# Input projection of a hybrid pooling and DeltaNet block: seven half-size products per 256 weight columns in place of eight

## The chip, the core and the metric

The kernel runs on one core of a Trainium2 chip. The metric is the device time of one execution in microseconds (us). Each engine of the core works through its own instruction stream in order: TensorE (PE; its weight loads are listed as PEld), VectorE (DVE), ScalarE (ACT), GpSimd (POOL) and SyncE (SP), which here only issues DMAs. They meet at semaphores.

## What is computed

The reference runs one layer over 528 positions (16 learned meta tokens ahead of 512 tokens) of width 2048, all in float32. Cut to what matters:

```
xn = rmsnorm(h, norm_w)
proj = xn @ w_in                      # 528 x 2048 times 2048 x 14368
u_pool, z_pool, q, k, v, z_dn, b, a, gate_pool, gate_dn = split(proj)
y_pool = causal_multiscale_pool(u_pool, pool_mix, pool_scale) * silu(z_pool)
qkv    = causal_depthwise_conv_silu(concat(q, k, v), conv_w)    # 4 taps
y_dn   = chunk_gated_delta_rule(l2norm(q), l2norm(k), v, beta, g), then gated rmsnorm with silu(z_dn)
merged = sigmoid(gate_pool) * (y_pool @ w_pool_out) + sigmoid(gate_dn) * (y_dn @ w_dn_out)
out    = rmsnorm((h + merged @ w_o)[16:], final_norm_w)
```

The column groups of the projection are u and z of the pooling branch (1024 each), q, k, v and z of the delta branch (2048 each, 16 heads of 128), and two gates (2048 each).

## The kernel before

**Precision.** Every large product is made of three passes in a rounded float32 form: each operand is a high part plus a low part, and TensorE adds high times high, low times high and high times low. xh and xl hold the high and low parts of the normalised x, [128, 16, 528] each, transposed. Of the weights wh and wl hold the two parts. ACT makes a high part (a copy, `split_hi`, L868) and DVE the low one (raw minus high, `split_lo`, L1208).

**Input projection.** It goes in 56 blocks of 256 weight columns: for each of four pooling groups a u and a z block (8), for each of eight pairs of heads a k, q, v and z block (32), and 16 gate blocks. One block loads 2048 x 256 weights in two DMAs of 1 MB, and `window` (L530 does each matmul) runs four windows: two halves of 128 output channels by two halves of 1024 rows, each of eight row tiles. A tile is three passes. The z and gate blocks want only 512 positions and take one matmul of 512 columns for each pass; u, k and v take 256 and 272 (or 256 and 260 for q) columns, since 528 don't fit one bank. That is 96 or 192 matmuls in a block. Weights are split in pieces of two row tiles, two windows (48 or 24 matmuls) ahead of their use.

**Between the matmuls** lie hooks, one after every two row tiles. Through them all engines carry the delta rule of pair d (`delta(d, m)`, m from 0 to 52) while the projection of pair d+1 runs; that of the last pair runs under the first four gate blocks. Its steps come in this order: decay factors, the Gram matrices of k (m = 3, 4), 16x16 block inverses on DVE alone (m = 14 to 18, lines L1427 to L1443, called W here), the assembly of the inverse of each chunk (m = 29 to 34), the recurrence over four chunks (m = 35 to 46), output norms (m = 48 to 52). The convolution is four DVE operations of 528 columns for each head of k, q and v (`convolve`, L1373 and L1376), and silu follows on ACT. POOL fetches the row sums of the gates for pair d (L1720, L1722), subtracts (L1731), later stores the result zst of the pair (L1735), and at once goes on to the rows of the next pair.

**After the projection** come two stages that the change leaves as they are but for addresses and the first loads: B, eight steps of 144 matmuls of 512 columns with the branch outputs, and C, 768 matmuls with w_o, then residual and norm.

## Time and profile before

| | us |
|---|---|
| runs (median of 3; lowest, highest) | 1962.79 (1962.67, 1963.48) |
| profiled execution: span from first to last instruction | 1960.8 |
| PE busy in the span | 1931.4 (99%) |
| DVE busy | 921.4 (47%) |
| ACT busy | 726.0 (37%) |
| granted TensorE clock, mean | 0.997 |

The profiled execution is known by its span; the time of a run also holds what lies around the span, and the median is 2.0 us above it. Matmuls overlap in the listing: one of 512 columns is listed with some 390 ns, but the next starts sooner. So the spacing of starts gives the price, not the mean duration. The page of the profile has busy times, the chain that ended last and the costliest groups; the views of the trace give rows for a stretch of time.

### The profile page before, as it was taken

Reading aid. Unit: us, or ns where it says so; the run is one execution under the profiler, and the core shown is the slowest. Engines: PE = TensorE matmul, PEld = TensorE weight load, DVE = VectorE, ACT = ScalarE, POOL = GpSimd, SP = SyncE. Lnnn points to the kernel's source line nnn. Section 1 sums busy time; section 2 is a strip of 40 time slices with the busy share of each in tenths; the row PEclk is TensorE's granted clock in tenths of the full one; section 3 lists DMA queues with packets and bytes.
Section 4 is the critical chain, followed back from the end, with each engine's and each line's share of the span. In section 5 each row is a group of like instructions: output and inputs, shape, how many; then the busy total and the mean of one; then the engine's idle time right before and its main releaser. Section 6 shows DMA issues by size and latency. Waiting matters only on the chain.

```text
span 1960.8 us, 35753 instructions
## 1 busy us (share of the span) xinstructions
PE 1931.4 (99%) x13729; PEld 1724.3 (88%) x13729; DVE 921.4 (47%) x2315; ACT 726.0 (37%) x2136; POOL 78.3 (4%) x105
## 2 busy tenths in 40 slices
PE   5999999999999999999999999999999999999998
PEld 5888899999999999999999988888888888888886
DVE  6333343656556466555646654322224444335332
ACT  5422223435353443535345353323234322224232
POOL 4000000000000000000000000000000000000000
PEclk8999999999999999999999999999999999999999
DMA  6133342433333242333334144333443534347302
GB/s 222 59 103 102 102 134 88 119 95 86 95 120 90 87 124 69 96 111 100 91 107 123 44 131 127 119 107 128 134 162 134 186 118 139 118 139 279 108 22 86
DMA packets 221302, 225.73 MB, mean 115 GB/s; under 512 B 33665, under 2 KB 197978, under 8 KB 220522
## 3 DMA queue, kind: packets, MB, share of 16 engines
q1 hardware_dynamic: 158898, 180.17, 28.1%
q10 hardware_dynamic: 55944, 22.63, 4.6%
q0 software_dynamic: 6336, 21.08, 3.4%
q8 instruction: 102, 1.67, 0.4%
q14 instruction: 22, 0.18, 0.0%
HBM read 199.65 MB, written 25.30 MB: 115 GB/s over the span
## 4 chain that ended last, share of the span: by engine, by line
PE 97%; ACT 1%; DVE 1%; issue 0%; POOL 0%; DMA 0%; ACTq 0%; SPq 0%; DVEq 0%
PE pj L530 82%; PE pg L530 10%; PE pt L530 3%; PE pt L679 1%; PE pg L781 0%; POOL xl L1696 0%; DVE fst L1233 0%; ACT xsquare L908 0%; DMA xt<-in_meta_tokens 0%; PE pj L574 0%; DVE xl L1239 0%; ACT wh L868 0%; DVE xt L1246 0%; ACT L1041 0%; ACT L1070 0%
## 5 line engine op out<-in xcount | busy, mean ns | idle before, releaser
L530 PE MATMUL pj<-xh,wh 128*128 128x512 f32 (+3 forms) x2688 | 735.1, 328 | 3.2 <-DVE wl L1208 3.1
L530 PE MATMUL pj<-xh,wl 128*128 128x512 f32 (+3 forms) x2688 | 712.4, 319 | 0.0
L530 PE MATMUL pj<-xl,wh 128*128 128x512 f32 (+3 forms) x2688 | 712.3, 319 | 0.0
L1208 DVE TENSOR_TENSOR wl<-raw,wh 128x256 fp32r<-128x256 f32 x896 | 344.2, 421 | 603.0 <-ACT wh L868 601.5
L530 PEld LDWEIGHTS pj<-xh,wh 128*128 128x128 f32 x2688 | 446.9, 189 | 43.2 <-DVE wl L1208 3.4
L530 PEld LDWEIGHTS pj<-xh,wl 128*128 128x128 f32 x2688 | 448.4, 188 | 35.9
L530 PEld LDWEIGHTS pj<-xl,wh 128*128 128x128 f32 x2688 | 448.8, 189 | 33.9 <-issue 1.0
L868 ACT ACTIVATE wh<-raw 128x256 fp32r<-128x256 f32 x896 | 307.0, 410 | 64.7 <-issue 45.0
L868 ACT ACTIVATE wh<-rawb 128x256 fp32r<-128x256 f32 (+1 forms) x224 | 85.0, 437 | 217.0 <-PE pj L530 189.8
L530 PE MATMUL pj<-yl,wh 128*128 128x512 f32 x384 | 149.5, 389 | 0.0
L530 PE MATMUL pj<-yh,wl 128*128 128x512 f32 x384 | 149.5, 389 | 0.0
L530 PE MATMUL pj<-yh,wh 128*128 128x512 f32 x384 | 149.4, 389 | 0.0
L1559 DVE TENSOR_TENSOR wl<-rawb,wh 128x256 fp32r<-128x256 f32 x192 | 69.5, 419 | 94.6 <-ACT wh L868 94.6
L1376 DVE SCALAR_TENSOR_TENSOR stg<-xin,convcur,stg 128x528 f32<-128x528 f32 x144 | 109.4, 760 | 0.2
L868 ACT ACTIVATE xin<-pj 128x512 f32<-128x512 f32 (+2 forms) x128 | 34.1, 336 | 154.3 <-PE pj L530 131.5
L1070 ACT ACTIVATE stg<-pj 128x512 f32<-128x512 f32 x32 | 19.1, 598 | 184.9 <-PE pj L530 184.9
L530 PEld LDWEIGHTS pj<-yl,wh 128*128 128x128 f32 x384 | 72.1, 188 | 15.1
L530 PEld LDWEIGHTS pj<-yh,wl 128*128 128x128 f32 x384 | 72.1, 188 | 15.0
L530 PEld LDWEIGHTS pj<-yh,wh 128*128 128x128 f32 x384 | 72.1, 188 | 14.8
L1026 ACT ACTIVATE oo<-pt,cur 128x128 f32<-128x128 f32 x64 | 20.0, 364 | 155.7 <-PE pt L530 155.7
L1582 DVE TENSOR_TENSOR gst<-gst,pj 128x512 f32<-128x512 f32 x32 | 20.6, 683 | 53.0 <-PE pj L530 53.0
L1735 POOL DMA_DIRECT2D branch_scratch<-zst x8 | 6.0, 745 | 905.4 <-DVE zst L1528 905.4
(243 smaller groups left out, 1784.3 us busy)
## 6 DMA issues: line engine op xcount, KB each, us to landing
raw<-in_w_in SPq DMA_DIRECT2D x112, 1024.0 KB, 6.2
rawb<-in_w_dn_out SPq DMA_DIRECT2D x16, 1024.0 KB, 6.3
rawb<-in_w_o SPq DMA_DIRECT2D x12, 1024.0 KB, 5.3
gates_scratch<-stg ACTq DMA_DIRECT2D x32, 256.0 KB, 2.1
rawb<-in_w_pool_out SPq DMA_DIRECT2D x8, 1024.0 KB, 5.7
gst<-gates_scratch POOLq DMA_DIRECT2D x32, 256.0 KB, 3.1
yraw<-branch_scratch SPq DMA_DIRECT2D x1, 5632.0 KB, 23.1
xt<-in_x SPq DMA_DIRECT2D x4, 1024.0 KB, 6.2
```

The costliest lines, as they stand in the source:

```text
L530: return pe.matmul(dst, lhs, rhs, start=start, stop=stop)
L679: mm = pe.transpose(pt[rows, i * P:(i + 1) * P], src, ident)
L868: return act.activation(dst, src, ACT.Copy)
L1026: act.activation(oo[:, at, :], pt[:, h * HD:(h + 1) * HD], ACT.Copy, scale=cur[:, EG, at:at + 1]).then_inc(o_inter, 1)
L1070: act.activation(gates_sb[c], pj[c][:, 0, :], ACT.Sigmoid).then_inc(proj_evac, 1)
L1208: tt(wl[:, j, 2 * q:2 * q + 2, :], raw[:, 2 * par + h, 2 * q:2 * q + 2, c * P:(c + 1) * P], wh[:, j, 2 * q:2 * q + 2, :].bitcast(F32), ALU ...
L1376: dve.scalar_tensor_tensor(acc, xin[:, src_tap:src_tap + T], w, acc, ALU.mult, ALU.add).then_inc(conv_step, 1)
L1559: tt(bwl[:, u, 2 * q:2 * q + 2, :], rawbs[u][:, 2 * q:2 * q + 2, c * P:(c + 1) * P], bwh[:, u, 2 * q:2 * q + 2, :].bitcast(F32), ALU.subtr ...
L1582: tt(gst[c][:, i, :], gst[c][:, i, :], pj[c][:, i, :], ALU.mult).then_inc(mg_step, 1)
L1735: pool.dma_start(y_d[bass.ds(PW + CW * d, CW), :].rearrange("(h e) t -> e h t", e=P), zst[:, :, :]).then_inc(y_stored, 16)
```

## The change

**Arithmetic.** x is cut in halves by position (two of 264: 8 meta tokens and 256 tokens) and by input row (two of 1024), a block's weights in halves by row and by column. Seven products of halves give the four quarters of the output. For the x side seven sums or halves (xh, xl of each: [128, 8, 264]) are made once at the start. For the weight side DVE makes four sums of 1024 columns in each block (`s1` to `s4`), in place in five raw slots, which are loaded in four DMAs of 512 KB with rows of 512 bytes. Each product is two chunks of four row tiles, each of 12 matmuls of 264 columns (260 for q, 256 for z and gates). One of the seven belongs to the next block (NEXT) and serves two quarters; the first block does eight products, the last six. The order of products in a block is 1, 4, 6, 2, 5, NEXT, 3.

**Splits.** wh and wl are now a ring of four chunks of 512 columns. ACT's and DVE's step t of a block splits chunk t + 3 (AHEAD = 3), and may start when chunk t - 1 has left TensorE.

**Outputs.** Three partial sums are copied from PSUM by ACT (snap), and DVE combines bank and copy into quarters (`c21`, `c22`, `c11`); ACT takes the fourth quarter from the bank. The hooks are 28 in a block: delta step m stands at hook 15m/8 of the pair's 112.

**Heads.** xin and stg hold one head at a time in place of three kinds. After convolution and silu ACT stores each head to DRAM (`head_store`), and SP loads kq, vch and zst of the pair back (4, 2 and 2 heads of 264 KB). vch, zst and the row sums share the place of tm, so POOL waits for the store of zst before it fetches the next rows. qk takes the place of dec, oo that of mk, and the scratch of W lies in st.

**The gate tables** (beta and decay) are made under pooling group 1 in place of group 0. The rest is as before.

```diff
+NEXT = 0
+ORDER_FIRST = (1, 2, 7, 6, 4, 5, NEXT, 3)
+ORDER = (1, 4, 6, 2, 5, NEXT, 3)
+ORDER_LAST = (1, 4, 6, 2, 5, 3)
+AHEAD = 3
+RINGS = 4
...
+SLOT_OF = {1: 0, 2: 1, 3: 1, 4: 3, 5: 3, 6: 4, 7: 4, NEXT: 4}
+RA, RB, RC, RF, RE = range(5)
+def base_of(b):
+    return 0 if isinstance(b, int) and b == 0 else 14 * b + 2
...
-            def window(cp, c, h, half, hook):
...
-                        pe.wait_ge(*((x_lo, 13), (x_lo, 14), (x_lo, 15), (x_lo3, 5))[kt // 4])
-                    for w, xx, first, last in ((wh, xh, True, False), (wh, xl, False, False), (wl, xh, False, True)):
-                        for dst, c0, n in halves:
-                            mm = product(dst, w[:, slot, k, :], xx[:, kt, c0:c0 + n],
-                                         first and kt == 0, last and kt == KT - 1)
-                    if k == UK - 1:
-                        mm.then_inc(pe_piece, 1)
-                    if k % 2 == 1:
-                        hook(k // 2)
...
+            def block_products(b, par, kind, kind_next, hook):
+                order, base = order_of(b), base_of(b)
+                first = isinstance(b, int) and b == 0
+                for i, what in enumerate(order):
+                    if what == 1:
+                        need(pe, last_done, b - 1)
+                    elif what == 2:
+                        need(pe, add_done, 3 * b)
+                    elif what == 4:
+                        pe.wait_ge(snap_done, snapped(b, "s4"))
+                    elif what == 6:
+                        pe.wait_ge(snap_done, snapped(b, "s1"))
+                    elif what == 5:
+                        pe.wait_ge(snap_done, snapped(b, "s2"))
+                    elif what == 3:
+                        pe.wait_ge(add_done, added(b, "C22"))
+                    elif what == NEXT:
+                        pe.wait_ge(add_done, added(b, "C21"))
+                    c0 = c0_of(kind_next if what == NEXT else kind)
+                    bank = bank_a[par] if what in (1, 6, 5, 3) else bank_c if what == 2 else bank_b
+                    opens, closes = what in (1, 2, 7, NEXT), what in (3, 2, 4)
+                    for h in range(2):
+                        chunk = 2 * i + h
+                        slot = (chunk + (0 if first else 2 * par + 2)) % RINGS
+                        if first and what in (1, 2):
+                            pe.wait_ge(x_lo_pool, chunk + 1)
+                        elif first and what != NEXT:
+                            pe.wait_ge(x_lo, {7: 1, 6: 3, 4: 5, 5: 7, 3: 9}[what] + h)
+                        pe.wait_ge(lo_done, base + chunk + 1)
+                        for k in range(HK):
+                            kt = HK * h + k
+                            for w, xx, one, last in ((wh, xh, True, False), (wh, xl, False, False), (wl, xh, False, True)):
+                                mm = pe.matmul(bank[:, c0:TH], w[:, slot, k, :], xx[what][:, kt, c0:TH],
+                                               start=opens and one and kt == 0, stop=closes and last and kt == KH - 1,
+                                               skip_group_check=True)
+                            if k == HK - 1:
+                                mm.then_inc(pe_chunk, 1)
+                            if k % 2 == 1:
+                                hook(2 * chunk + k // 2)
...
-            def split_lo(cp, par, j, q):
-                c, h = j // 2, j % 2
-                dve.wait_ge(hi_done, 16 * cp + 4 * j + q + 1)
-                tt(wl[:, j, 2 * q:2 * q + 2, :], raw[:, 2 * par + h, 2 * q:2 * q + 2, c * P:(c + 1) * P],
-                   wh[:, j, 2 * q:2 * q + 2, :].bitcast(F32), ALU.subtract).then_inc(lo_done, 1)
...
+            def split_lo(b, par, t):
+                if not has_target(b, t):
+                    return
+                of, what, half, chunk, slot = split_target(b, par, t)
+                dve.wait_ge(hi_done, chunk + 1)
+                tt(wl[:, slot, :, :], raw[:, SLOT_OF[what], HK * half:HK * (half + 1), :], wh[:, slot, :, :].bitcast(F32),
+                   ALU.subtract).then_inc(lo_done, 1)
...
+            def s2(b):
...
+                tt(raw[:, RE, :, :], raw[:, RE, :, :], raw[:, RF, :, :], ALU.add).then_inc(sum_done, 1)
...
+            def s1(b):
...
+                tt(raw[:, RF, :, :], raw[:, RC, :, :], raw[:, RF, :, :], ALU.add).then_inc(sum_done, 1)
...
+            def s4(b):
...
+                tt(raw[:, RB, :, :], raw[:, RB, :, :], raw[:, RE, :, :], ALU.add).then_inc(sum_done, 1)
...
+            def s3(b):
...
+                tt(raw[:, RE, :, :], raw[:, RA, :, :], raw[:, RC, :, :], ALU.add).then_inc(sum_done, 1)
...
+            def c21(b, kind, dst):
+                order = order_of(b)
+                dve.wait_ge(snap_done, snapped(b, "s2"))
+                dve.wait_ge(pe_chunk, base_of(b) + max(after(order, 4), after(order, 6)))
+                for part, cols in placed(kind, 0, dst):
+                    ins = tt(part, bank_b[:, cols], snap[:, 1, cols], ALU.subtract)
+                ins.then_inc(add_done, 1)
...
+            def block_steps(b, par, kind, dst, free, event, hook):
+                order = order_of(b)
+                first, last = 7 in order, NEXT not in order
+                for t in range(2 * len(order)):
+                    if t == (3 if first else 0):
+                        s2(b)
+                    if t == (7 if first else 1):
+                        s1(b)
+                    if t == (8 if first else 5):
+                        s4(b)
+                    if not last and t == (9 if first else 6):
+                        s3(b + 1)
+                    split_lo(b, par, t)
+                    if t == (10 if first else 7):
+                        free(1)
+                        c21(b, kind, dst[1])
+                    if t == (12 if first else 10):
+                        c22(b, par, kind, dst[1])
+                    event(t)
+                    if t == (13 if kind in ("k", "q", "v") or first else 12 if kind == "u" else 11):
+                        free(0)
+                        c11(b, kind, dst[0])
+                    hook(2 * t)
+                    hook(2 * t + 1)
...
+            def head_store(p, k, c):
+                act.wait_ge(head_silu, 8 * p + 2 * k + 2 - c)
+                act.dma_start(head_d[bass.ds(p, 1), 2 * k + c, :, :].rearrange("a p t -> (a p) t"), stg[:, c, :]).then_inc(head_stored[c], 16)
...
+            row_differences(0)
+            with pool.Fori(1, PAIRS) as d:
+                head_out(d - 1)
+                pool.wait_ge(y_stored, 16 * d)
+                row_differences(d)
+            head_out(PAIRS - 1)
```

Three places show how the streams move. First TensorE at a block boundary in the pooling stage, before (L530 is every large matmul; pj is a bank of the projection):

```order
L530 MATMUL pj<-xl,wh 128x512
L530 MATMUL pj<-xh,wl 128x512
L632 REGISTER_ALU
L632 COMPARE_AND_BRANCH
L530 MATMUL pj<-xh,wh 128x256 [waits proj_evac,lo_done]
L530 MATMUL pj<-xh,wh 128x272
L530 MATMUL pj<-xl,wh 128x256
L530 MATMUL pj<-xl,wh 128x272
```

and now, in a k block, where chunk 9 ends and the product for the next block begins (L701 is the matmul of `block_products`, L832 a transpose of the delta rule):

```order
L701 MATMUL pj<-xh,wh 128x264 [waits lo_done]
L701 MATMUL pj<-xl,wh 128x264
L701 MATMUL pj<-xh,wl 128x264
L139 REGISTER_ALU
L832 MATMUL pt<-cst,tm 128x128 [waits tok_done]
L832 MATMUL pt<-cst,tm 128x128 x3
L701 MATMUL pj<-xh,wh 128x264
L697 REGISTER_ALU [waits add_done]
L701 MATMUL pj<-xh,wh 128x260 [waits lo_done]
```

Matmuls of 512 and of 256 with 272 columns have become matmuls of 256 to 264, and a wait for a split comes every 12 of them.

Second DVE in W, before (oo holds the 16x16 blocks, each step multiplies and subtracts; wl is a split):

```order
L1437 TENSOR_TENSOR oo<-oo 66x54 [waits w_step]
L1440 TENSOR_TENSOR oo<-oo 66x6x9 [waits w_prod]
L1208 TENSOR_TENSOR wl<-raw,wh 128x256 [waits hi_done]
L1437 TENSOR_TENSOR oo<-oo 66x56 [waits w_step]
L1440 TENSOR_TENSOR oo<-oo 66x7x8 [waits w_prod]
```

and now (raw<-raw is the weight sum `s1`, stg the first tap of a convolution):

```order
L1855 TENSOR_TENSOR st<-st 66x54 [waits w_step]
L139 REGISTER_ALU
L1858 TENSOR_TENSOR st<-st 66x6x9 [waits w_prod]
L1491 REGISTER_ALU [waits raw_loaded2]
L1493 TENSOR_TENSOR raw<-raw 128x1024 [waits lo_done,sum_done]
L1474 REGISTER_ALU
L1475 TENSOR_TENSOR wl<-raw,wh 128x512 [waits hi_done]
L1793 TENSOR_SCALAR stg<-xin,convcur 128x528 [waits head_stored0,last_done,add_done]
L1855 TENSOR_TENSOR st<-st 66x56 [waits w_step]
```

Where one split of 256 columns stood between two parts of W, a sum of 1024 columns, a split of 512 and a tap stand now.

Third POOL at the end of a pair, before:

```order
L1731 ISA [waits rowg_loaded]
L1731 TENSOR_TENSOR dec<-tm,table 128x1024
L1732 ISA
L1732 TENSOR_TENSOR dec<-tm,table 16x32
L1734 ISA
L1735 ISA [waits y_ready]
L1735 DMA branch_scratch<-zst 128x2x512
L1727 REGISTER_ALU
L1727 COMPARE_AND_BRANCH
```

and now:

```order
L2180 ISA [waits y_ready]
L2180 DMA branch_scratch<-tm 128x2x512
L2185 REGISTER_ALU
L2164 ISA [waits y_stored]
L2164 DMA tm<-gate_sum_scratch 128x1024
L2166 ISA
L2166 DMA tm<-gate_sum_scratch 16x2x16
L2173 ISA
L2175 ISA [waits rowg_loaded]
L2175 TENSOR_TENSOR dec<-tm,table 128x1024
```

Between the store of one pair and the fetch for the next stands a wait for the store.

## Rows read from the trace of the kernel before

**Rows 1.** The page, busy time of each engine.
```profile
PE 1931.4 (99%) x13729; PEld 1724.3 (88%) x13729; DVE 921.4 (47%) x2315; ACT 726.0 (37%) x2136; POOL 78.3 (4%) x105
```

**Rows 2.** The page, chain that ended last, by engine.
```profile
PE 97%; ACT 1%; DVE 1%; issue 0%; POOL 0%; DMA 0%; ACTq 0%; SPq 0%; DVEq 0%
```

**Rows 3.** That chain in order of time: start, length, what.
```profile
90.46 45.24 PE pj L530 x288
...
1240.35 538.60 PE pj L530 x2376
```

**Rows 4.** Timeline of PE in a q block: start, length of the pair.
```profile
269.88 0.40 PE L530 MATMUL pj<-xh,wl 128*128 128x256 f32 x2
...
271.28 0.40 PE L530 MATMUL pj<-xh,wl 128*128 128x256 f32 x2
```

**Rows 5.** One pair in steady state: PE, PEld, DVE, ACT, POOL busy, clock, DMA share.
```profile
574.75:690.42 115.67, 115.67 (x1118) 110.06 (x1118) 67.95 (x181) 49.67 (x162) 3.93 (x5) 1.00 0.33 98
```

**Rows 6.** Groups by line (one pair; rawb: stage C): busy, mean ns, idle before.
```profile
L1208 DVE TENSOR_TENSOR wl<-raw,wh 128x256 fp32r<-128x256 f32 x64 | 25.7, 420 | 35.8 <-ACT wh L868 35.6
...
L1376 DVE SCALAR_TENSOR_TENSOR stg<-xin,convcur,stg 128x528 f32<-128x528 f32 x18 | 13.7, 760 | 0.0
...
L1590 DVE TENSOR_TENSOR wl<-rawb,wh 128x512 fp32r<-128x512 f32 x32 | 21.4, 688 | 35.0 <-ACT wh L868 35.0
L868 ACT ACTIVATE wh<-rawb 128x512 fp32r<-128x512 f32 x32 | 19.6, 627 | 40.8 <-PE pt L530 21.6 <-PE pj L530 19.2
```

**Rows 7.** Timeline of DVE in W and just before it.
```profile
579.18 1.23 DVE L1418 TENSOR_TENSOR mk<-mk,qd 128x1024 f32<-128x1024 f32 x1
580.32 0.17 DVE L1419 TENSOR_TENSOR mk<-mk,qd 16x32 f32<-16x32 f32 x1
...
591.72 0.28 DVE L1427 TENSOR_SCALAR oo<-oo 66x256 f32<-66x256 f32 x1
...
593.37 0.42 DVE L1208 TENSOR_TENSOR wl<-raw,wh 128x256 fp32r<-128x256 f32 x1
593.71 0.20 DVE L1437 TENSOR_TENSOR oo<-oo 66x44 f32<-66x44 f32 x1
...
601.22 0.76 DVE L1376 SCALAR_TENSOR_TENSOR stg<-xin,convcur,stg 128x528 f32<-128x528 f32 x1
```

**Rows 8.** Timeline of POOL at the end of a pair.
```profile
666.76 0.74 POOL L1735 DMA_DIRECT2D branch_scratch<-zst  x1 [105.30 <-DVE zst L1528]
667.59 0.56 POOL L1720 DMA_DIRECT2D tm<-gate_sum_scratch  x1
...
677.06 0.23 POOL L1732 TENSOR_TENSOR dec<-tm,table 16x32 f32<-16x32 f32 x1
```

**Rows 9.** DMA issues: count, KB, median us to landing.
```profile
raw<-in_w_in SPq DMA_DIRECT2D x112, 1024.0 KB, 6.2
branch_scratch<-zst POOLq DMA_DIRECT2D x8, 512.0 KB, 4.1
```

**Rows 10.** Timeline of DVE in the prologue, L1239 a low part of x, L1233 transposed x.
```profile
20.10 1.75 DVE L1239 TENSOR_TENSOR xl<-fst,xh 128x512 fp32r<-128x512 f32 x1
...
26.71 1.75 DVE L1239 TENSOR_TENSOR xl<-fst,xh 128x512 fp32r<-128x512 f32 x1
...
31.55 1.32 DVE L1239 TENSOR_TENSOR xl<-fst,xh 128x512 fp32r<-128x512 f32 x1 [0.69 <-ACT xh L868]
32.79 2.59 DVE L1233 TENSOR_TENSOR fst<-pj,vcol 128x512 f32<-128x512 f32 x4
```

**Rows 11.** First matmuls on PE (timeline), and the granted clock of that stretch (windows).
```profile
35.81 0.81 PE L530 MATMUL pj<-xh,wh 128*128 128x256 f32 x2 [3.11 <-DVE wl L1208]
37.30 0.64 PE L530 MATMUL pj<-xh,wh 128*128 128x256 f32 x2
37.74 0.64 PE L530 MATMUL pj<-xl,wh 128*128 128x256 f32 x2
...
35.80:38.00 2.20, 2.19 (x10) 2.19 (x11) 2.20 (x2) 2.20 (x8) 2.20 (x2) 0.51 0.04 11
```

More of the change, by code:

```diff
@@ new lines, in build @@
+        raw = lay.tensor("raw", [5, KH, P])
+        wh = lay.tensor("wh", [RINGS, HK, P], F32R)
+        wl = lay.tensor("wl", [RINGS, HK, P], F32R)
+        snap = lay.tensor("snap", [3, TH])
+        lay.close()
+        qk = dec[:, 0:XC]
+        oo = mk[:, 0:XC].rearrange("p (n e) -> p n e", e=HD)
+        vch = tm[:, :].rearrange("p (h t) -> p h t", h=2)
+        zst = tm[:, 0:2 * SEQ].rearrange("p (h t) -> p h t", h=2)
+        rr, vn, junk, vnm = work[:, 0], work[:, 1], work[:, 2], work[:, 3]
@@ L244, in build @@
         lay = layout(2)
-        lay.skip_to(at_xt)
         ba = lay.tensor("ba", [T])
@@ new lines, in free, with hook @@
+                    def free(c, k=k):
+                        if k == 3:
+                            dve.wait_ge(head_stored[c], 16 * (4 * p + 3))
+                        else:
+                            need(dve, conv_step, (6 * p + 2 * k + 1 - c) * 4)
+                    def hook(h, k=k):
+                        m = delta_step(28 * k + h)
+                        if d is not None and m is not None:
+                            delta(d, m)
+                    dst = [xin[:, TAPS - 1:]] * 2 if k < 3 else [stg[:, c, :] for c in range(2)]
```

1045 lines of the change are left out of this document (662 added, 383 removed).

## The prediction

> **What bounds the kernel now.** I read the busy times first: TensorE is busy for 99% of the span, VectorE for 47%, ScalarE for 37% [rows 1]. The chain of waits agrees: 97% of what ended last is TensorE [rows 2], in long unbroken stretches, 45.24 us for 288 matmuls and 538.60 us for 2376 [rows 3]. So time can be saved only by taking columns off TensorE, and the saving stays only while DVE and ACT keep ahead of it. The windows show how much room an average pair has: in 115.67 us PE is busy for all of it, DVE for 67.95, ACT for 49.67, at full clock [rows 5].
>
> **Price of a matmul.** The spacing of starts counts. 512 columns: 538.60 / 2376 = 226.7 ns. The block with 256 and 272 columns: (45.24 - 96 x 0.2267) / 192 = 122.3 ns, mean 264 columns [rows 3]. In the q block 12 matmuls of 256 and 260 start in 271.28 - 269.88 = 1.40 us, 116.4 ns [rows 4]. A single length of 264, 260 or 256 doesn't occur alone; I take 121.5, 118 and 117 ns. Bounds: 118.9 to 122.3, 117.2 to 120.6, and 115.6 to 119.0 (from the halves of 226.7 and from columns times 0.45 or 0.463 ns).
>
> **TensorE's share.** Before: 20 blocks of u, k, v with 192 are 3840 x 122.3 ns, 8 of q 1536 x 116.4, 28 of zp, z, gate 2688 x 226.7: 1257.8 us. Now 168 in each block: 3360 x 121.5, 1344 x 118, 4704 x 117 = 1117.2 us (1100.8 to 1132.8). **-140.6 us** (-125 to -157), where 7/8 of 1257.8 would be 1100.6, but short matmuls cost a little more for each column.
>
> **What DVE gets for it.** Operations follow each other at the listed time less 0.08 us: 1.23 listed, next start 1.14 later [rows 7]. So a weight sum of 1024 columns costs 1.14 us, a split of 512 0.61 (688 ns listed), where two splits of 256 cost 0.68; a convolution tap 0.68 [rows 6]. Per block 4 sums (4.6), 14 splits (8.5, before 10.9), 3 combinations of about 0.35. In a pair that makes some 97 us of DVE work. TensorE needs 4 x 168 matmuls, 80.3 us, and as before the delta rule's 115.67 - 91.2 = 24.5: 104.8 us. The average fits. ACT gets to some 70 us. But splits now lie 3 chunks ahead, about 4.4 us, where they lay two windows, some 11 us, ahead. A burst of DVE work that was covered now stops TensorE. I walk through the pair for bursts.
>
> *W, at the turn from k to q.* From 591.72 to the tap at 601.22 DVE spends 9.5 us, 1.36 in four splits (0.34 each, 593.37 to 593.71) and 1.1 in two taps: W itself is 7.0 us [rows 7]. In the new order, from the last tap of k to the split of chunk 6 of q, DVE also has, counted out: taps 0.68 + 0.41 + 0.68, one combination 0.35, sums 2 x 1.14, splits 4 x 0.61 = 6.8. With W 13.8 us, begun 1.3 into q: the split of chunk 6 is done at 15.1. TensorE wants it at 6 x 12 x 0.118 + 2.5 for delta matmuls = 11.0. Until chunk 9 two more sums, two taps, three splits and 0.3 of hand-offs follow: 20.9 against 15.3. Stall **5.6 us**.
>
> *The row differences.* POOL issues the store at 666.76, the row load at 667.59, and ends its subtraction at 677.29: 10.5 us [rows 8]. Now it waits for the store to land, 4.1 us [rows 9], and then takes 677.29 - 667.59 = 9.7: 13.8. The last delta step stands at hook 97, so y is ready some 9.5 us before the z block ends (14 hooks of 0.70 less 0.3). The differences are there 4.3 us into the next k block. DVE waits for them with the later splits queued behind: dec 1.24, three sums 3.4, six splits to chunk 9 3.7, the Gram and mask steps some 4.9, hand-offs with a square-root table load on ACT some 2.5, so 20.0 us against TensorE's 9 x 1.46 + 4.5 = 17.6. Stall **2.5**.
>
> *Rest.* Assembly, recurrence and the z block, which shares DVE with the norms: **2.0**, an estimate from the same counting, bounds 0 and 8.8 (third rival). That is 10.1 a pair, 70.7 for seven; pair 0, without a delta rule, 0.5; the last pair under gates 6.5. **+77.7 us**. The pair so comes to 104.8 + 10.1 = 115, as before.
>
> *Prologue.* Before, the last transposed x ends at 35.4, with three low parts, 1.75 + 1.75 + 1.32 = 4.8, in between [rows 10]; these go behind, so 30.6. Then DVE has for block 0, up to the combination that the last product wants: 8 sums and 10 low parts of 1056 columns (1.17, from 1.14 for 1024) 21.1, 16 splits 9.8, 5 weight sums 5.7, combinations and pooling 2.5: 38 us. Last product 2.9. That is 71.5, and 3 for matmuls at half clock: after 3.11 us idle the first ones show a granted clock of 0.51, the 1.2 GHz level, and 220 ns each (37.30 to 37.74 for two) [rows 11]. 74.5 against 35.8 + 2 + 23.3 = 61.1: **+13.4** (bounds +7, if the sums hide some of each other, and +22, if the clock stays low all through).
>
> *Into the branch stage.* In the last gate block DVE has 9 splits, 3 sums, 3 combinations, 16 low parts of y at a split's price and 8 splits of 256: 22.3 us; TensorE has 144 x 0.117 = 17. With a lead of 2: **+3.5**. Pooling and gate blocks: DVE 14.2 of 19.7 us, no term. Stores and loads of the heads are 264 KB each beside a DMA share of 0.33 [rows 5], and a head is wanted most of a pair later: no term; without that cover each would cost its 4 us landing [rows 9]. The gate tables under group 1 lie in the same slack, likewise nothing.
>
> **Sum.** -140.6 + 13.4 + 77.7 + 3.5 = -46. Against the profiled execution's span of 1960.8 that is 1915; the median is 2.0 above it, so **1917 us**. A measurement here tells 0.2% (4 us) from no change.
>
> **Rivals.**
> (a) *The cover holds.* The lead of three chunks swallows the bursts, as DVE's average of 97 in 104.8 allows, and only prologue and transition remain: 1917 - 77.7 = **1839**. Against it stands the count in W, where DVE simply has 20.9 us for TensorE's 15.3. Chance 0.14.
> (b) *Each stall drops the clock.* After 3.11 us idle 264 columns cost 220 ns rather than 122 for some time [rows 11]. Two stalls in each of eight pairs, with some 20 matmuls at 98 ns more each, 1.9 us: +30, **1947**. For it: those rows; against it: single waits below 3 us. "TensorE: Matmul & The Clock Gate" of the Trainium skill (Part 1) says that throttled is the default and activity releases it; the first matmuls' 0.51 agrees. Chance 0.08.
> (c) *Slower: the hand-to-hand steps.* The assembly and the recurrence, m = 29 to 46, are 18 steps in which TensorE, DVE and ACT hand to each other. Before, a step could meet a split of 0.34 ahead of it; now a sum of 1.14 or a split of 0.61 on DVE, and one of 0.55 (627 ns listed) on ACT [rows 6, 7]. If each is held for 0.6 us and its matmul stands at the head of TensorE's queue, that is 10.8 a pair instead of 2.0: +8.8, times 8 = +70, **1987**. It turns the result slower from +46 / 8 = 5.7 us a pair. For it: hooks come 7/8 apart where the steps' latency stays; against it: between steps still stand six matmuls, 0.7 us. Chance 0.18.
> (d) *The weights come late.* The same packets as before, now of 512 bytes, carry 512 KB. If they cost twice, a load takes 12.4 us where 1 MB took 6.2 [rows 9]; loads start only when a chunk frees its slot, so s3 comes some 3 us late in each of 56 blocks: +168, **2085**. Chance 0.05. "DMA: Bandwidth & Descriptors" of the Trainium skill ("Why small descriptors are slow") gives some 3 cycles fixed for each packet beside 32 bytes a cycle; by that estimate 16 + 3 against 32 + 3 cycles, 3.4 us a load, and this rival falls. No row here has such rows, so the small chance stays.
>
> **Chances.** Forecast 0.55, (a) 0.14, (b) 0.08, (c) 0.18, (d) 0.05. Faster: 0.52 of the forecast, 0.14 of (a), 0.07 of (b), 0.73. Slower: 0.17 of (c) and (d), 0.22. The tails left of each lie within 0.2%: 0.05. Range: the forecast's own terms give 1885 to 1950 (matmul price 16, prologue 7, pair stalls 25, in quadrature); for eight in ten it reaches to 1870 towards (a) and over (b) and (c) to 1990.
>
> **What would show it.** Right: 264 columns spaced 121.5 ns, 256 ones 117; a pair of about 115 us; PE idle, released by a split on DVE, near chunks 6 to 9 of q and chunk 9 of k; block 0 ending near 74.5 us; DVE waiting for dec some 4 us into k. Wrong: idle of PE spread over steps 29 to 46 (c), PE waiting for sums that wait for raw loads (d), a granted clock well below 1 in the pairs (b), or no idle at all (a).

## The result and the profile after

The changed kernel takes **2041.28 us** (median of 4 runs, 2038.36 to 2049.55) against 1962.75: 1.0405 times the kernel before, 95% interval 1.0383 to 1.0427. It is slower by 4%, where 1917 was forecast and 1990 was the end of the range.

The page of the changed kernel, busy times and the chain by engine, which answer to [rows 1] and [rows 2]:

```profile
PE 1862.6 (91%) x15073; PEld 1741.3 (85%) x15073; DVE 1435.5 (70%) x2628; ACT 953.8 (47%) x2148; POOL 70.3 (3%) x94
...
PE 62%; DVE 16%; issue 9%; DMA 6%; ACT 4%; ACTq 2%; DVEq 1%; SPq 0%; POOLq 0%; POOL 0%
```

TensorE is no longer the bound by itself: nearly two fifths of the chain lie on others, 9% of it in "issue", time in which an engine waited for nothing that the profile shows.

To see where the time went, both traces are cut at the starts of the same blocks; idle time ahead of a block's first matmul counts to that block. The windows give start and end, length, the busy time of PE, PEld, DVE, ACT and POOL (and how many instructions), granted clock, DMA share and GB/s. Before:

```profile
0.00:69.87 69.87, 49.43 (x348) 48.25 (x349) 39.35 (x82) 35.03 (x69) 22.79 (x21) 0.93 0.52 167
69.87:241.79 171.92, 171.92 (x1000) 148.94 (x998) 61.93 (x155) 51.04 (x151) 4.94 (x7) 1.00 0.32 100
241.79:332.80 91.01, 91.01 (x673) 87.26 (x672) 38.23 (x91) 25.02 (x82) 5.08 (x9) 1.00 0.37 117
679.93:795.57 115.64, 115.64 (x1118) 110.05 (x1116) 67.95 (x180) 49.63 (x162) 3.93 (x5) 1.00 0.33 99
1256.54:1495.90 239.36, 239.36 (x1058) 198.21 (x1056) 60.97 (x176) 69.70 (x198) 0.00 (x0) 1.00 0.44 145
1495.90:1517.82 21.92, 21.92 (x98) 18.18 (x97) 15.35 (x32) 14.68 (x34) 0.00 (x0) 1.00 0.06 24
```

After, the same stages (block 0; blocks 1 to 7; pair 0; one steady pair; eleven gate blocks; the last block):

```profile
0.00:77.15 77.15, 45.81 (x274) 42.92 (x275) 61.89 (x81) 39.90 (x54) 14.19 (x10) 0.87 0.41 120
77.15:252.32 175.17, 168.27 (x1289) 159.31 (x1288) 129.80 (x212) 81.97 (x152) 4.95 (x7) 0.98 0.36 100
252.32:334.42 82.10, 81.66 (x675) 80.91 (x673) 76.44 (x114) 43.13 (x82) 5.66 (x9) 1.00 0.56 159
706.99:833.64 126.65, 112.08 (x1116) 107.76 (x1116) 102.30 (x202) 65.36 (x161) 3.93 (x5) 0.96 0.44 124
1333.14:1551.82 218.68, 218.68 (x1851) 218.68 (x1850) 165.40 (x232) 119.19 (x222) 0.00 (x0) 1.00 0.50 133
1551.82:1591.20 39.38, 21.87 (x147) 21.50 (x145) 22.47 (x40) 17.76 (x38) 0.00 (x0) 0.74 0.58 203
```

The arithmetic does what was promised where nothing disturbs it: a gate block takes 218.68 / 11 = 19.88 us in place of 21.76. Undisturbed matmuls start 118.3 ns apart with 256 columns, 119.7 with 260 and 121.2 with 264. Over all blocks that is worth 133 us. It is given back, and 76 more (all rows of the table are from the two profiled executions):

| stage | before | after | saved on TensorE | lost | forecast loss |
|---|---|---|---|---|---|
| prologue and block 0 (7.7 us of gate matmuls moved out) | 62.2 | 77.2 | 0.3 | 15 | 13.4 |
| blocks 1 to 7 (without those 7.7) | 171.9 | 167.5 | 17 | 12 | 0 |
| pair 0 | 91.0 | 82.1 | 10 | 2 | 0.5 |
| seven pairs | 810.2 | 876.6 | 73 | 139 | 70.7 |
| last pair under gates | 113.5 | 122.1 | 8 | 16 | 6.5 |
| eleven gate blocks | 239.4 | 218.7 | 21 | 0 | 0 |
| last block | 21.8 | 39.4 | 5 | 22 | 3.5 |
| the rest | 443.1 | 445.6 | 0 | 2 | 0 |

By blocks, a steady pair's k, q, v and z take 33.5, 31.9, 36.5 and 23.4 us (means of seven; before, 29.6, 26.9, 36.5 and 22.8). TensorE idles 4.6, 6.5, 1.4 and 1.0 us in them, where before it never idled. (The recorded expectations below cut one product, 24 matmuls or 2.8 us, too early. So they have 33.6, 29.9, 36.6 and 25.1 for the four, and 42.4 for the last block.) What TensorE waited for (us in total, times, longest):

```profile
PE pj L701 <- DVE wl L1475: 42.4, 33, 11.3
PE pj L701 <- issue: 24.6, 6, 4.2
PE pt L832 <- ACT pt L1216: 23.2, 8, 3.1
PE pj L701 <- DVE xin L1531: 15.2, 7, 2.5
...
PE pg L666 <- issue: 9.5, 8, 3.5
```

Six waits of "issue" of 4 us each, ahead of the large matmul, are new. They stand at the head of the k block in the last six of the seven pairs, that is, wherever the pair loop jumps back. The first of the seven has no jump ahead of it, and its row differences were made long before: its k block takes 27.5 us, the other six 34.3 to 34.9. The timeline at one of them, TensorE first (L701 is the large matmul), then ScalarE, VectorE and GpSimd:

```profile
706.71 0.28 PE L701 MATMUL pj<-xh,wl 128*128 128x256 f32 x1
711.00 0.58 PE L701 MATMUL pj<-xh,wh 128*128 128x264 f32 x1 [4.01 <-issue]
711.38 0.42 PE L701 MATMUL pj<-xl,wh 128*128 128x264 f32 x1
711.60 0.42 PE L701 MATMUL pj<-xh,wl 128*128 128x264 f32 x1
```

```profile
711.97 0.63 ACT L1026 ACTIVATE wh<-raw 128x512 fp32r<-128x512 f32 x1 [5.73 <-issue]
```

```profile
706.27 0.69 DVE L1475 TENSOR_TENSOR wl<-raw,wh 128x512 fp32r<-128x512 f32 x1 [0.73 <-ACT wh L1026]
712.09 1.22 DVE L1486 TENSOR_TENSOR raw<-raw 128x1024 f32<-128x1024 f32 x1 [5.13 <-issue]
...
717.12 1.23 DVE L1807 TENSOR_TENSOR dec<-dec,cst 128x1024 f32<-128x1024 f32 x1 [3.01 <-POOL dec L2176]
```

```profile
700.41 0.74 POOL L2180 DMA_DIRECT2D branch_scratch<-tm  x1 [109.67 <-DVE tm L1946]
708.69 0.56 POOL L2164 DMA_DIRECT2D tm<-gate_sum_scratch  x1 [7.54 <-DMA branch_scratch<-tm]
...
714.99 1.90 POOL L2175 TENSOR_TENSOR dec<-tm,table 128x1024 f32<-128x1024 f32 x1 [5.15 <-DMA tm<-gate_sum_scratch]
```

Three engines stand still together, from about 707 to 711 or 712, each right behind its own jump back of the pair loop. Then VectorE waits 3.01 us more for the row differences: the store of y was issued 6.6 us ahead of the k block, not 9.5, and took 7.54 us to land, not 4.1 [rows 9]. And the matmuls behind the stop are spaced by 220 ns: the 1.2 GHz level, granted clock 0.51 here:

```profile
710.00:717.00 7.00, 6.00 (x27) 6.01 (x28) 2.01 (x4) 3.12 (x5) 2.02 (x2) 0.51 0.52 176
```

In the q block the largest wait is for ScalarE, in the fourth chunk: 3.1 us for the squares of q (L1216) in every pair. ScalarE itself had stood 2.86 us for a weight sum of VectorE, and then loaded a table:

```profile
749.40 0.66 PE L832 MATMUL pt<-cst,kq 128*128 128x128 f32 x4 [3.09 <-ACT pt L1216]
```

```profile
745.63 0.63 ACT L1026 ACTIVATE wh<-raw 128x512 fp32r<-128x512 f32 x1 [2.86 <-DVE raw L1486]
746.28 1.28 ACT L1181 ACT_TABLE_LOAD   x1
```

### The profile page after: what moved, and what is told of

It is laid out like the page before. It is cut to its first block, busy times and chain, and to the rows that moved or that the text cites. A ratio compares the mean times of both kernels' runs of the same rounds, so it can differ in the third digit from the quotient of the medians.

```text
span 2036.8 us, 40992 instructions
## 1 busy us (share of the span) xinstructions
PE 1862.6 (91%) x15073; PEld 1741.3 (85%) x15073; DVE 1435.5 (70%) x2628; ACT 953.8 (47%) x2148; POOL 70.3 (3%) x94
## 4 chain that ended last, share of the span: by engine, by line
PE 62%; DVE 16%; issue 9%; DMA 6%; ACT 4%; ACTq 2%; DVEq 1%; SPq 0%; POOLq 0%; POOL 0%
PE pj L701 34%; PE pj L666 16%; PE pg L666 9%; DVE wl L1475 4%; PE pt L666 3%; DMA branch_scratch<-tm 2%; DVE stg L1796 2%; ACT wh L1026 2%; DMA tm<-gate_sum_scratch 2%; DMA yraw<-branch_scratch 1%; DVE st L1855 1%; DVE st L1858 1%; DVE raw L1508 1%; DVE raw L1499 1%; PE pt L832 1%
## 5 line engine op out<-in xcount | busy, mean ns | idle before, releaser
L701 PE MATMUL pj<-xh,wh 128*128 128x256 f32 (+2 forms) x3136 | 936.1, 299 | 92.9 <-DVE wl L1475 42.4
L701 PE MATMUL pj<-xl,wh 128*128 128x256 f32 (+2 forms) x3136 | 903.0, 288 | 0.0
L701 PE MATMUL pj<-xh,wl 128*128 128x256 f32 (+2 forms) x3136 | 901.6, 288 | 0.0
L1026 ACT ACTIVATE wh<-raw 128x512 fp32r<-128x512 f32 x784 | 484.9, 629 | 605.8 <-PE pj L701 423.7
L701 PEld LDWEIGHTS pj<-xh,wh 128*128 128x128 f32 x3136 | 611.1, 195 | 112.4 <-issue 54.0
L1475 DVE TENSOR_TENSOR wl<-raw,wh 128x512 fp32r<-128x512 f32 x784 | 534.8, 687 | 193.4 <-ACT wh L1026 187.6
L701 PEld LDWEIGHTS pj<-xl,wh 128*128 128x128 f32 x3136 | 612.6, 195 | 1.0 <-issue 1.0
L701 PEld LDWEIGHTS pj<-xh,wl 128*128 128x128 f32 x3136 | 609.9, 194 | 0.0
L666 PE MATMUL pj<-yh,bwh 128*128 128x512 f32 x384 | 149.8, 390 | 1.4 <-DVE yl L2010 1.4
L1486 DVE TENSOR_TENSOR raw<-raw 128x1024 f32<-128x1024 f32 x56 | 68.3, 1220 | 31.0 <-issue 30.9
L1493 DVE TENSOR_TENSOR raw<-raw 128x1024 f32<-128x1024 f32 x56 | 68.4, 1222 | 3.7
L1499 DVE TENSOR_TENSOR raw<-raw 128x1024 f32<-128x1024 f32 x56 | 68.2, 1218 | 2.1
L1508 DVE TENSOR_TENSOR raw<-raw 128x1024 f32<-128x1024 f32 x56 | 68.1, 1216 | 0.8 <-DMA raw<-in_w_in 0.8
## 6 DMA issues: line engine op xcount, KB each, us to landing
yraw<-branch_scratch SPq DMA_DIRECT2D x1, 5120.0 KB, 20.6
```

The lines of the kernel that those rows point to most:

```text
L666: return pe.matmul(dst, lhs, rhs, start=start, stop=stop)
L701: mm = pe.matmul(bank[:, c0:TH], w[:, slot, k, :], xx[what][:, kt, c0:TH], start=opens and one and kt == 0, stop=closes and last and kt == ...
L1026: return act.activation(dst, src, ACT.Copy)
L1475: tt(wl[:, slot, :, :], raw[:, SLOT_OF[what], HK * half:HK * (half + 1), :], wh[:, slot, :, :].bitcast(F32), ALU.subtract).then_inc(lo_don ...
L1486: tt(raw[:, RE, :, :], raw[:, RE, :, :], raw[:, RF, :, :], ALU.add).then_inc(sum_done, 1)
L1493: tt(raw[:, RF, :, :], raw[:, RC, :, :], raw[:, RF, :, :], ALU.add).then_inc(sum_done, 1)
```

## Experiments

Theories at the start: the k block's stop is **instruction fetch** after the jump, or **weight loads** held up by the loads of k and q and the stores beside them; the surplus of a pair is **VectorE's load**, its **order** (W, the row differences), or the **clock**. All runs below were timed against the kernel before, 1962.9 to 1963.3 us in the same sessions.

One thing blurs the comparisons. In the changed kernel's profile all seven v blocks take 36.2 to 36.9 us. In most of the other profiles some v blocks take 39 to 48, with the granted clock at 1.2 GHz for 3 to 24 us while TensorE is busy nearly throughout. A stretch of the longest one in the seven pairs, in run 1:

```profile
399.00:418.00 19.00, 19.00 (x155) 17.29 (x152) 8.07 (x16) 2.66 (x6) 0.00 (x0) 0.50 0.14 43
```

Such a block costs 2 to 11 us. What sets it off is not shown. So a difference of some 10 us between two runs needs the blocks of both to be read.

**1. Without the jump.** On TensorE, ScalarE and VectorE:

```diff
-            with pe.Fori(1, PAIRS) as p:
+            for p in range(1, PAIRS):
                 pair_blocks(p, p - 1)
```

> The pair loop is written out seven times for TensorE, ScalarE and VectorE in place of a loop, so no engine jumps back. Theory 1 (the stop of 4.0 us on TensorE, 5.8 on ScalarE and 5.1 on VectorE at the start of each k block is instruction fetch after the jump): six such stops go, and with each the half-clock stretch of 6.8 us after it, 6 x (4.1 + 3.4) = about 45 us, so some 1996 us. Theory 2 (the stop is a weight load held up by the loads of k and q, the store of y and the head stores at the same time): the stops stay where they are, and the time stays within 5 us of 2041.

Measured: 2040.65 us (2033.16 to 2044.88), no change. But not because the stop stayed: none of the three engines stops there any more. TensorE's waits of this run:

```profile
PE pt L832 <- ACT ktok L1212: 45.4, 7, 6.6
PE pj L701 <- DVE wl L1475: 39.2, 22, 11.3
```

A wait for ktok of up to 6.6 us has taken the place of the 4 us stop, in the same block: ScalarE's ktok stands behind its exponentials of dec, and these behind the differences. The stop is the jump's, and the row differences lie under it. By blocks of the profiles, k takes 34.6 to 36.4 us in the six pairs, as with the jump; the q blocks gain 17 us together, and v blocks at the lower clock lose 19.

**2. Row differences ahead of the store.** GpSimd fetches the rows into st, which is free once the last solve of the pair is through. The load of vch (`load_vch` on SyncE) now waits for the store of y in place of the differences:

```diff
-                head_out(d - 1)
-                pool.wait_ge(y_stored, 16 * d)
+                pool.wait_ge(tr_mm, NCH * d)
+                pool.wait_ge(qkv_mm, NCH * d)
                 row_differences(d)
+                head_out(d - 1)
```

> The rows of gate sums go into st, and GpSimd makes the differences before the store of y, so nothing waits for that store. If the wait for the store sets the k block, VectorE's 3 us wait for dec and what follows in ScalarE go, up to 8 x 3 = 24 us: 2017 to 2025. If the stop at the loop's jump covers most of it (the differences come 5 us after VectorE resumes), 2025 to 2035. If the differences were hidden, 2041.

Measured: 2052.36 us (2045.55 to 2057.19), 11 us slower than the changed kernel. The wait for dec is gone, the jump's stop (24.3 us in six) is not, and k takes 32.9 to 34.4 us in the six pairs. Something is new in the z block. A weight sum on VectorE, 1.22 us elsewhere, takes 2.92 or 2.93 in all seven pairs where GpSimd's subtraction lies over it (two views of this run, VectorE and GpSimd):

```profile
833.27 2.92 DVE L1499 TENSOR_TENSOR raw<-raw 128x1024 f32<-128x1024 f32 x1
```

```profile
832.69 2.43 POOL L2175 TENSOR_TENSOR dec<-st,table 128x1024 f32<-128x1024 f32 x1 [5.05 <-DMA st<-gate_sum_scratch]
835.09 1.21 POOL L2176 TENSOR_TENSOR dec<-st,table 16x32 f32<-16x32 f32 x1
```

In the changed kernel GpSimd's subtraction falls where VectorE stands waiting for it, so this costs nothing there. It makes each z block 1.5 us longer, 10 us in all. The larger loss of this profile is another: four v blocks at the lower clock take 39.8 to 43.0 us, 22 us together, while k and q blocks gain 8.

**3. Light sums.** Seven eighths of each weight sum from block 1 on left out.

```diff
-                tt(raw[:, RE, :, :], raw[:, RE, :, :], raw[:, RF, :, :], ALU.add).then_inc(sum_done, 1)
+                tt(raw[:, RE, 0:few(b), :], raw[:, RE, 0:few(b), :], raw[:, RF, 0:few(b), :], ALU.add).then_inc(sum_done, 1)
```

> Leaves out seven eighths of each weight sum from block 1 on (128 of 1024 columns are summed, so the products are of other numbers). VectorE has 4 x 1.0 us less in each block. If VectorE's bursts set the pair's surplus, the waits for wl and for the quarters go, at 20 us of surplus a pair perhaps 8 to 10 of it, and some 5 in the pooling stage: 1950 to 1980. If the stops are of instructions and DMA, the time falls by less than 20 us.

Measured: 1976.74 us (1974.71 to 1980.39), 64.5 less. Pairs fall from 125.2 to 117.8 us (means), and blocks 1 to 7 get back 6 us. One pair of this run:

```profile
676.72:794.52 117.80, 108.57 (x1117) 105.17 (x1116) 87.94 (x202) 65.12 (x161) 3.98 (x6) 0.99 0.47 135
```

So 14 us less busy time on VectorE is worth 7.5 us in a pair, with the stop still in it (20.6 us in six).

**4. Branch outputs in pieces.** The profile of the changed kernel shows the next stage's load of 5 MB issued only behind the last weight load, 3 us ahead of the last block (SP), and TensorE there:

```profile
1548.49 0.38 SPq L568 DMA_DIRECT2D yraw<-branch_scratch  x1
```

```profile
1571.77 0.55 PE L701 MATMUL pj<-xh,wh 128*128 128x256 f32 x1 [11.28 <-DVE wl L1475]
```

Before, that load was issued 38 us ahead of the last block; weight slots now come free one chunk at a time, so the last weight load is late, and all that SP has queued behind it. The edit waits for the stores of y ahead of the last four gate blocks and puts five tiles of the load behind the weight loads of each:

```diff
+                    n = 5 * (2 * (i - NGATE // 2 + 2) + k)
+                    sp.dma_start(yraw[:, n:n + 5, :], y_rows[:, n:n + 5, :]).then_inc(yraw_loaded, 16)
```

> The 5 MB of branch outputs for the next stage are loaded in four pieces between the weight loads of the last four gate blocks, in place of one load behind the last weight load. TensorE's 17.5 us idle in block 55 goes: 2041 - 18 to 20 = 2021 to 2024. If the low parts of y on VectorE set that block anyway (the term of 3.5 us), some 4 us of idle stay: 2025.

Measured: 2031.08 us (2030.11 to 2031.75), 10 less. The last block falls from 39.4 to 26.7 us. In this profile one block of the last pair, 47.8 us in place of 39.3 with the clock low for 24 us, hides part of that. The second wait in the last block (6.3 us for a quarter that VectorE makes behind low parts of y) stays, as run 11 shows by removing it.

**5. Edits 1 and 2 together.**

> Both earlier edits together: the pair loop written out, and the gate-sum rows through st with the differences ahead of the store of y. Theory A (two waits lie over each other at the start of each pair, and each alone is covered by the other): now both go, and with them the half-clock stretch of 6.8 us, so k blocks fall from 33.6 to about 28 us, less some 4 us that the differences cost in the z block: 7 x (5.5 - 4) + 6 = about 2020 to 2030; up to 2005 if the z block's loss is less. Theory B (the start of a pair waits for something else, such as the load of k and q): 2040 or more.

Measured: **1988.00 us** (1986.17 to 1993.36), 1.0135 times the kernel before (1.0118 to 1.0152) and 53 less than the changed kernel, where one edit alone gave 1 and the other cost 11. Five of the seven k blocks now take 27.2 us, like the undisturbed first one of the changed kernel (mean 27.8, from 33.5). A pair of this run reads:

```profile
686.12:803.45 117.33, 110.27 (x1118) 106.50 (x1117) 103.81 (x203) 65.30 (x161) 5.15 (x5) 0.97 0.47 134
```

**6. Without W.** 13 of W's 14 steps left out.

```diff
+                        if j > 1:
+                            continue
                         tt(own, wblk[:, 0:j, j:j + 1].broadcast_to([NBLK, j, rest]),
```

> Leaves out 13 of the 14 steps of the 16x16 block inverses on VectorE (the changed kernel otherwise). VectorE has about 6.5 us less at the turn from k to q. If W is what q's waits come from (forecast: 5.6 us a pair), the q block falls from 29.9 to 25 to 26 us and the start of v by up to 2: 2041 - 8 x 5.6 = 1996, range 1985 to 2005. If ScalarE's order or the clock sets the q block, less than 15 us.

Measured: 2015.62 us (2012.42 to 2019.62), 25.7 less: 3.2 a pair. q blocks fall from 31.9 to 27.8 us, 4.0 a pair; two v blocks at the lower clock (39.9 and 42.9 us) take some of it back. TensorE still idles 4.2 us in q, so W is one cause of that idle time and not the whole.

**7. W spread**, on run 5:

```diff
-        NSTEP = 3
+        NSTEP = 2
...
-                if m == W0 + 5:
+                if m == W0 + 8:
...
-                if m == W0 + 10:
+                if m == W0 + 12:
```

> As the run with both edits, with W in 7 pieces of two steps in place of 5 of three, and ScalarE's store and loads of the inverses 3 and 2 steps later, so that ScalarE does not stand for W's end with splits behind it. If W's density and ScalarE's 4.2 us wait for it set the q block, 8 x 3 to 4 us less than the run with both edits. If only the sum of VectorE's work in the block counts: within 5 us of it.

Measured: 1987.83 us (1982.36 to 1994.06): nothing. In the profiles q is 1.1 us shorter than in run 5 and v 2.4 longer. Four of the seven v blocks (39.9 to 45.0 us) lie at the lower clock for 7 to 17 us; whether the later loads of the inverses bring that on is not shown.

**8. Run 5 with light sums.**

> As the run with both edits, and seven eighths of each weight sum left out. VectorE then has 4.2 us less in each block and no stop at the pair's start: the pair would come down to TensorE's 105.3 us and a few waits, 108 to 112, and the time to 2041 - 65 - 8 x 6 = about 1930, range 1915 to 1955. If it stays above 1960, something other than VectorE and the pair's start carries most of the surplus.

Measured: 1926.28 us (1925.42 to 1927.23), 0.981 of the kernel before (0.9794 to 0.9827): the one run that beats the kernel before, and it leaves out work. One pair, with VectorE at 89 us of 112:

```profile
664.62:776.77 112.15, 107.82 (x1118) 105.08 (x1117) 89.47 (x203) 65.47 (x161) 4.47 (x5) 0.98 0.49 140
```

**9. Quiet loop**, on the changed kernel; from the second pair on the delta rule sees only 4 new positions of each k and q:

```diff
+                n = T if d == 0 else 4
-                sp.dma_start(kq[:, :, :, :].rearrange("p a h t -> p (a h) t"),
+                sp.dma_start(kq[:, :, :, 0:n].rearrange("p a h t -> p (a h) t"),
```

> The changed kernel with its loop, and the load of k and q (1056 KB, 8.4 us) cut to 8 KB from the second pair on (4 positions of each head, so the delta rule works on old numbers). If the stop after the jump back is long because the instruction fetches stand behind these loads, it shrinks from 4.0 us on TensorE and 5.1 on VectorE to under 1, and the time falls by some 6 x 5 = 30 us where the wait for dec doesn't take its place. If the stop is the plain latency of fetching code that no longer lies at hand, it stays at 4 to 5 us and the time within 10 us of 2041.

Measured: 2038.71 us (2032.38 to 2043.47), not to be told from the changed kernel. VectorE's stop stays, at 6.2 to 6.6 us, and ScalarE's at 5.8 to 6.7:

```profile
717.32 2.35 DVE L1487 TENSOR_TENSOR raw<-raw 128x1024 f32<-128x1024 f32 x1 [6.48 <-issue]
```

So the loads of k and q do not cause these two. TensorE's stop is another matter: it falls from 24.6 us in six to 10.9, at most 2.2 us each. What it gains there it loses at the Gram products of the same block, to a wait that again names no releaser (21.6 us in place of 9.5):

```profile
PE pg L667 <- issue: 21.6, 10, 3.6
PE pj L702 <- DVE xin L1532: 15.0, 7, 2.7
PE pj L702 <- issue: 10.9, 6, 2.2
```

The records of the instruction queue q8 show why. After each of TensorE's six jumps a packet of 16 KB starts on it, and none within 7 us of the last pass's end, where nothing jumps.

| us after TensorE's jump | packet of q8 starts | TensorE's next instruction | TensorE idle |
|---|---|---|---|
| kernel before | 0.9 to 1.6 | 3.4 to 4.0 | 0 |
| changed kernel | 3.3 to 3.5 | 5.9 to 6.2 | 4.0 to 4.2 |
| run 10 | 3.4 to 4.0 | 5.9 to 6.5 | 4.0 to 4.6 |
| this run | 0.9 to 1.5 | 3.3 to 4.1 | 1.4 to 2.2 |

In the meantime TensorE works off some 16 matmuls that stand ahead of the jump. They had 512 columns before, 16 x 0.227 = 3.6 us, and it never idled. Now they have 256, 16 x 0.118 = 1.9 us, and what is left is the stop. So the shorter matmuls of the change uncover some 2 us of it, and the load beside it adds some 2 more.

**10. TensorE alone keeps its loop** (run 5 otherwise).

> As the run with both edits (1988.0 us), but TensorE keeps its loop; ScalarE and VectorE are written out. If each engine stops by itself at its own jump, TensorE's 4.0 us stop stays in full, six times, with half clock behind it: 6 x (4.0 + 3.4 x 0.5) = +34, about 2020. If the stop is the other engines' (the trace before this run names no releaser for TensorE's), it goes: 1988.

Measured: 2021.22 us (2013.65 to 2023.11), 33 more than run 5. Six stops are back, on TensorE only:

```profile
PE pj L701 <- issue: 25.2, 6, 4.6
```

Each engine has its own stop at its own jump. 25.2 us of idle cost 33. The other 8 fit the matmuls at half clock around the end of each stop (3.4 or 6.8 us at that level), but no run separates them.

**11. Best of the edits.** Run 5, the y pieces, and in the last block the quarter made ahead of four low parts and eight splits:

```diff
-                if t in (9, 10):
+                if t in (10, 11):
                     for q in range(4):
-                        split_b(0, t - 9, q)
+                        split_b(0, t - 10, q)
```

> Both edits, the y loads in four pieces, and in the last gate block VectorE makes the quarter that TensorE waits for (6.3 us there) ahead of four low parts of y and eight splits. 1988 - 12.5 (block 55 from 42.4 to about 30) - 6 = about 1970, range 1962 to 1978: near the kernel before.

Measured: 1975.25 us (1973.53 to 1978.05); the last block takes 23.0 us, where its 144 matmuls need 17.0. Still 1.0068 times the kernel before (1.0051 to 1.0085).

**12. Filled idle time.** Run 5, and on TensorE ahead of the second transposes of q:

```diff
+                if m == W0 + 4:
+                    wait(mq_ready, 3, 3)
+                    for i in range(24):
+                        product(pg[2][:, 0:TH], xh[1][:, 0, 0:P], xh[1][:, 0, 0:TH], True, True)
```

> As the run with both edits, with 24 matmuls of 264 columns (2.9 us) into an unused bank on TensorE where it idles 3.1 us in each q block for ScalarE's squares of q. They add work and shorten nothing but the idle time. If idle time costs also by the lower clock after it (rival b of the forecast), the half-clock stretch behind them goes and 8 x 1.7 = 13 us are gained: 1975. If the clock falls for other reasons, 1988 or a little more.

Measured: 1985.30 us (1978.93 to 1988.97), 3 less, within the spread of the two. The waits for pt are gone; those for wl rise from 43.9 to 49.5 us. TensorE idles 2.3 us in a q block in place of 4.4. The clock is up (0.980 against 0.975) and little is gained. That a faster TensorE only waits sooner for VectorE fits the wl waits, but is not shown: two v blocks at the lower clock (43.0 and 41.3 us) stand in this profile too.

**13 and 14. First tap on ScalarE**, on run 11, and with 22 filling matmuls:

```diff
-                    dve.tensor_scalar(acc, xin[:, src_tap:src_tap + T], w, None, ALU.mult).then_inc(conv_step, 1)
+                act.activation(stg[:, c, :], xin[:, 3:3 + T], ACT.Copy, scale=convcur[:, 3, which, c:c + 1]).then_inc(conv_step, 1)
```

> As the run with both edits, the y loads in pieces and the last gate block reordered (1975.3 us), and the first tap of each convolution made by ScalarE (a copy with a scale) in place of VectorE: six operations of 0.41 us less on VectorE a pair, six of some 0.65 more on ScalarE. If VectorE's load carries the pairs' remaining surplus, as the run with light sums says (16.8 us less on VectorE gave 7 to 8 a pair), 8 x 1.2 = 10 us are gained: 1965. If ScalarE's queue is as near to the limit, nothing or a loss of up to 10.

> The same with 22 idle-filling matmuls in each q block, which gave 3 us on the run with both edits: 1962, range 1955 to 1970. This is the best that these edits give together; below 1959 it would beat the kernel before.

Measured: 1974.90 us (1969.92 to 1978.69) and 1972.47 (1964.82 to 1978.54). Neither can be told from run 11. No version that does all the work beats the kernel before; the last stands at 1.004 (1.0025 to 1.0055).

**15 and 16. Longer loops in the kernel before.** Idle instructions (semaphore increments) at each hook of its pair loop, on three engines, and on VectorE alone:

```diff
                                 delta(d, 16 * k + 4 * j + q)
+                                if not isinstance(d, int):
+                                    dve.sem_inc(padv, 1)
```

> The kernel before, computing the same, with instructions that do nothing (increments of unused semaphores) in the body of its pair loop: 64 on TensorE, 64 on VectorE, 128 on ScalarE, so that each body is longer than in the changed kernel (by its instructions 1020 against 1005, 370 against 351, 329 against 285). If the stop after the jump back comes from the length of the bodies, it appears here as well, 4 to 6 us on each engine at six pair starts: 1963 + 30 to 50. If it comes from something else in the changed kernel, 1963 to 1967.

> The kernel before with the 64 idle instructions on VectorE alone. If length counts for each engine by itself, VectorE alone stops for 5 us at six pair starts, and TensorE, with its splits two windows ahead (some 11 us), doesn't notice: 1963 to 1966, with the stop to be seen in VectorE's rows. If length doesn't matter, no such stop.

Measured: 1969.39 us (1.0030 of the kernel before, 1.0019 to 1.0042) and 1963.36 (1.000). No stop of 4 us on TensorE. The instruction queue q14 does react (packets and MB, kernel before, run 15, run 16, changed kernel):

```profile
q14 instruction: 22, 0.18, 0.0%
```

```profile
q14 instruction: 83, 0.68, 0.1%
```

```profile
q14 instruction: 53, 0.43, 0.1%
```

```profile
q14 instruction: 88, 0.72, 0.1%
```

From 460 us to the end of the pair loop q14 carries no packet in the kernel before, 28 in run 16, 56 in run 15 and 58 in the changed kernel. With its body padded, VectorE (runs 15 and 16) and ScalarE (run 15) see a packet start some 1.0 us after each jump and go on 2.6 to 3.0 us after it, where it was 0.3 us before. So on these two engines a longer body is fetched anew in each pass. In the kernel before, VectorE idles 6.4 us around its jump and ScalarE 6.2, which hides most of such a stop in these runs. Why the stop is 5 to 6 us in the changed kernel and below 3 here stays open. TensorE makes its fetch with or without idle instructions (q8, run 9). It hardly stops in run 15, since the 16 matmuls ahead of the jump still have 512 columns and last 3.6 us, where its next instruction comes 3.4 to 3.9 us after the jump.

## Why the prediction was wrong

**Right.** TensorE's share: -133 measured, -140.6 forecast, inside its bounds (-125 to -157); 264 columns cost 121.2 ns against 121.5, 260 and 256 some 1.5 more than forecast. The gate stage needs no term. Block 0 ends at 77.2 us against 74.5; the forecast's own terms for VectorE add up to 39.1 and not 38, which gives 75.6. VectorE does wait for dec, though it gets it 10 us into k and not 4. Rival (d) is out: a weight load of 512 KB lands in 4.1 us. The Trainium skill's rule on small descriptors ("DMA: Bandwidth & Descriptors", "Why small descriptors are slow (HBM only)") gave an estimate of 3.4, and the trace agrees in kind.

**Near by luck.** The q block's stall was forecast at 5.6 us, for splits on VectorE at chunks 6 to 9, and TensorE idles 6.5 us in q. But 3.1 of these are the wait for ScalarE's squares in the fourth chunk, 2.2 the wait for a quarter ahead of the last product, and only 1.1 waits for splits. Without W (run 6) q is 4.0 us shorter.

**The step that failed** is the pair's sum of stalls, 10.1 us a pair, where 19.8 were lost (13.6 of it idle time of TensorE, at most 4.9 more the clock), and in it above all the k block, priced at 2.5:
- In six pairs k takes some 7 us more than the undisturbed 27.5, 42 us in all. Two waits of about the same length lie over each other there. One is the stop at the jump, which the forecast had not at all. The other is the row differences, whose start it had too early (store issued 6.6 us ahead of k and not 9.5, landing 7.5 and not 4.1). Removing either alone leaves k at 33 to 36 us (runs 1 and 2); removing both brings it to 27.2 and the time down by 53 us (run 5).
- The weight sums' average load. The text said that the average fits (97 in 104.8) and looked for bursts. VectorE measured 102.3, and taking 14 us of it away gives 7.5 a pair (run 3), most of it in k and q. That so little room makes each stall last longer is argued from this, not shown by itself.
- Rival (b), priced at 30 us with a chance of 0.08, came beside the forecast case, not in place of it. Over the seven pairs 14 stretches, 68 us together, show the 1.2 GHz level. Half of that, 34 us or 4.9 a pair, bounds the loss, near its price. The Trainium skill ("TensorE: Matmul & The Clock Gate", Part 1) says that the default is throttled and activity releases it. The stretches behind the stops agree. The v blocks of other runs, where the level stays low for up to 24 us with TensorE busy, don't fit it so simply.

**Terms that were taken as nothing.** Blocks 1 to 7 lost 12 us: in three of the four z blocks TensorE waits once for a split, 1.6 to 2.7 us, and light sums return 6 us. The last block lost 22, where 3.5 were forecast: the y load, not VectorE's 22.3 us of work, set it (runs 4 and 11 give back 16 of them together). For queues the forecast asked who is late with the weights, but not what SP has queued behind the last of them. The last pair under the gates lost 16 in place of 6.5; no run takes that apart.

**The slower rival** was the wrong one. (c) placed 10.8 us a pair in the hand-to-hand steps of v and z, where TensorE idles 2.4 us in all.

## What to carry to other kernels

Before shortening the work of the engine that bounds, look at what the others' idle time was paying for: here it hid a store's landing and a 5 MB load, and the long matmuls queued on TensorE hid the fetch at its loop's jump. An experiment that removes one wait and changes nothing doesn't acquit that wait; remove it together with its neighbour. Read such pairs of runs block by block, since a total can hide a gain in one block under a lower clock in another. And when an engine would be over 90% busy by the forecast's own count, as VectorE here, a sum of single bursts can be too small a price.

## What the runs showed of the hardware

- Jumping back in a long loop stops TensorE for 4.0 to 4.2 us, VectorE for 5.1 to 5.2 and ScalarE for 5.7 to 6.0 where no idle time covers it, each for itself (changed kernel, runs 1 and 10). Without the 1 MB load beside it TensorE's stop is 1.4 to 2.2 us, and that of the other two stays (run 9).
- TensorE's next instruction behind its jump came 3.3 to 4.1 us later without that load and 5.9 to 6.5 with it; some 16 matmuls ahead of the jump run in the meantime, so their length decides what is seen of it (kernel before, changed kernel, runs 9 and 10).
- A tensor operation on GpSimd holds up VectorE: 2.92 us in place of 1.22 for a sum in all seven pairs of run 2, and GpSimd's own small one 1.21 us in place of 0.23 [rows 8].
- Around the end of a 4 us stop the clock is at its lower level for 3.4 or 6.8 us, with 220 ns a matmul. It also stayed there for up to 24 us while TensorE was busy (runs 1 and 4).
